# First slab by contraction unit for all four row tiles, from an x laid out turned, behind 36 small matmuls

## The chip, the cores and the metric

One core of a Trainium2 chip runs the whole program. The metric is the device time of one execution in microseconds. TensorE does matmuls, VectorE and ScalarE do the elementwise work, SyncE and ScalarE issue the DMAs.

## The reference

Two transformer blocks run after one another on x (512 tokens x 1024, f32). What matters here is the head of the first block:

```
xn   = rmsnorm(x, attn_norm_g)              # x * rsqrt(mean(x*x)) * g, per token
proj = xn @ w_in                            # 1024 -> 2312 columns
qa, ka, va, qb, kb, vb, f_logit = split(proj, (512, 128, 128, 512, 512, 512, 8))
qa = rmsnorm(qa per head, q_norm_a);  ka = rmsnorm(ka per head, k_norm_a)
out_a = sliding-window attention of qa, ka, va in blocks of 128 queries
...                                         # second attention, out projection, MLP, second block
```

The per-token factor rsqrt(mean(x*x)) commutes with the product by w_in, so it can be applied to x or, later, to rows of proj.

## The kernel before

Every f32 product is done as three passes in fp32r: each operand is split into a high part (ScalarE copies it to fp32r) and the rest (VectorE subtracts), and TensorE adds high x high, high x low and low x high. Weights come in slabs of up to 512 columns, and a slab in four units `q` of two 128-row blocks (`raw[q]`, 512 KB). A unit is loaded by SyncE (`unit`, L465), its high part is made by ScalarE (`high_of`, L611), its low part by VectorE (`low`, L1702), and the latter's end (`unit_split`) also lets SyncE load the next slab's unit into the same buffer. `gemm_done` counts finished product tiles, `gemm_free` tiles whose bank has been read.

**The first stage**, which the change is about, computes eight tiles of proj, in the order of `FIRST` (L50), (slab, row tile). Slab 0 is qa (512 columns), slab 1 is ka, va and the forget logits (264 columns). At the start the gain vector is spread over the partitions by two f32 matmuls of ones (L1148). VectorE multiplies row tile 0 of x by it, TensorE turns the tile by 8 transposes (`turn_half`, L1124), and both splits are made of the turned tile (`xt_high` L630, `xt_low` L1693). Then `first_product` (L1157) multiplies tile 0 unit by unit as slab 0 arrives, and each further row tile is turned in the middle of the product before it (`between`, L1210). Row tile 0 is scaled late, by `root0`, the others by `first_rows` (L1710) before they are turned.

**After each of the eight tiles** come its heads, each engine in a written order. ScalarE squares the tile (`head_squares`, L664), VectorE sums per head (`head_means`, L1731), ScalarE takes a first root (`head_roots`, L676: a logarithm L680 and an exponential L681) and for slab 1 copies v and the logits (L716, L717), VectorE refines the root and scales the rows into `qn` (`head_rows`, L1740, ends with `gemm_free`). TensorE turns `qn` (`turn_heads`, L1196), and ScalarE stores the result with its gain (`head_gain`, L653, ends with `qk_stored`). In ScalarE's loop (L704) `head_gain(g - 3)` stands ahead of `head_squares(g)`. VectorE's last of these, `head_means(7)`, `maxima(0)` and `head_rows(7)`, stand behind its loop (L1929 to L1931).

**The main loop of the first block** has 70 halves in a fixed order on each engine. On TensorE its first instruction is `scores(0)` (L1254), the scores of the first head pair of query block 0, and what it waits for is not touched by the change:

```
if p == 0:
    pe.wait_ge(gemm_free, 6)
    ...
    pe.wait_ge(silu_step, SINK_STEPS)
...
    if h == 0:
        pe.wait_ge(qk_stored, max(FIRST.index((0, n)), FIRST.index((1, n))) + 1)
```

Behind it TensorE has `part_product` (L1229) of slab 2, three of 24 k steps to each half, and the remaining head turns.

## Time and profile before

| | us |
|---|---|
| median of 3 runs | 1192.47 (1192.09 to 1193.83) |
| span of the profiled execution | 1191.0 |
| TensorE busy | 1175.3 |
| VectorE busy | 702.9 |
| ScalarE busy | 485.0 |

The profiled execution's own time beside its span isn't given apart: the span is from the first to the last instruction, and the median of the runs lies 1.5 us above it. The chain of work that ended last is 91% TensorE. Busy time of TensorE is modelled, so the waits and the spacing of matmuls are read, not the busy share.

### The profile page before, as it was taken

How to read it: one execution, taken by the hardware profiler on the slowest of the kernel's cores; microseconds unless marked ns; L12 is line 12 of the kernel's file. 1: busy time of each engine (PE TensorE's matmuls, PEld its weight loads, DVE VectorE, ACT ScalarE, POOL GpSimd, SP SyncE). 2: the span in 40 equal slices, each digit the busy share in tenths (PEclk: the TensorE clock that was granted, in tenths of full speed). 3: DMA queues.
4: the chain of work that ended last, by engine and by line, in shares of the span. 5: the costliest groups of instructions: out<-in, count | busy, mean ns of one | idle time of the engine just before them, and what ended most of it. 6: DMA issues, size and time to landing. Idle time of an engine off the chain costs nothing.

```text
span 1191.0 us, 16691 instructions
## 1 busy us (share of the span) xinstructions
PE 1175.3 (99%) x6182; PEld 950.3 (80%) x6184; DVE 702.9 (59%) x1081; ACT 485.0 (41%) x874; POOL 24.7 (2%) x23
## 2 busy tenths in 40 slices
PE   8999999999999999999999999999999999999997
PEld 5877776688888888888888886578988888888886
DVE  7786567768777776753688235847633333333335
ACT  6655444535334334324541113845541532432431
POOL 0000000000000000000000003400000000000000
PEclk9999999999999999999999999999999999999999
DMA  6322211218667676644325221132333222223301
GB/s 228 124 72 71 72 36 54 72 64 284 223 213 241 207 254 208 213 145 142 123 72 174 85 71 46 54 126 71 108 105 106 98 97 89 106 88 93 119 19 71
DMA packets 76573, 144.27 MB, mean 121 GB/s; under 512 B 7347, under 2 KB 11315, under 8 KB 76500
## 3 DMA queue, kind: packets, MB, share of 16 engines
q1 hardware_dynamic: 54882, 99.12, 25.3%
q10 hardware_dynamic: 21618, 44.18, 11.6%
q8 instruction: 46, 0.75, 0.3%
q14 instruction: 27, 0.22, 0.1%
HBM read 140.36 MB, written 2.13 MB: 120 GB/s over the span
## 4 chain that ended last, share of the span: by engine, by line
PE 91%; DVE 5%; ACT 2%; issue 1%; DMA 0%; DVEq 0%; ACTq 0%
PE gemm L1091 25%; PE gemm L1093 25%; PE gemm L1092 25%; PE aux L1132 1%; PE aux L1338 1%; PE gemm L1378 1%; PE gemm L1379 1%; PE gemm L1380 1%; DVE nmax L2192 1%; PE aux L1091 1%; PE aux L1615 1%; PE gemm L1275 1%; PE aux L1093 1%; PE aux L1092 1%; PE gemm L1288 1%
## 5 line engine op out<-in xcount | busy, mean ns | idle before, releaser
L1091 PE MATMUL gemm<-xt_hi,w_hi 128*128 128x512 f32 (+1 forms) x704 | 254.4, 361 | 0.3 <-DVE xt_lo L1697 0.3
L1093 PE MATMUL gemm<-xt_hi,w_lo 128*128 128x512 f32 (+1 forms) x704 | 253.7, 360 | 0.0
L1092 PE MATMUL gemm<-xt_lo,w_hi 128*128 128x512 f32 (+1 forms) x704 | 253.5, 360 | 0.0
L1707 DVE TENSOR_TENSOR w_lo<-w_raw,w_hi 128x1024 fp32r<-128x1024 f32 (+1 forms) x176 | 208.0, 1210 | 31.0 <-ACT w_hi L840 26.3
L1091 PE MATMUL gemm<-w_hi,ht_hi 128*128 128x512 f32 (+1 forms) x512 | 198.9, 389 | 0.0
L1093 PE MATMUL gemm<-w_hi,ht_lo 128*128 128x512 f32 (+1 forms) x512 | 198.5, 388 | 0.0
L1092 PE MATMUL gemm<-w_lo,ht_hi 128*128 128x512 f32 (+1 forms) x512 | 198.3, 387 | 0.0
L840 ACT ACTIVATE w_hi<-w_raw 128x1024 fp32r<-128x1024 f32 x124 | 124.0, 1049 | 172.5 <-PE gemm L1093 127.9
L1091 PEld LDWEIGHTS gemm<-xt_hi,w_hi 128*128 128x128 f32 x704 | 132.7, 189 | 21.6 <-DVE xt_lo L1697 0.5
L1092 PEld LDWEIGHTS gemm<-xt_lo,w_hi 128*128 128x128 f32 x704 | 132.7, 188 | 20.1
L1093 PEld LDWEIGHTS gemm<-xt_hi,w_lo 128*128 128x128 f32 x704 | 132.7, 189 | 20.1
L2005 DVE TENSOR_TENSOR ht_lo<-hid,ht_hi 128x512 fp32r<-128x512 f32 x64 | 44.3, 692 | 171.0 <-ACT hid L853 171.0
L1091 PEld LDWEIGHTS gemm<-w_hi,ht_hi 128*128 128x128 f32 x512 | 96.2, 188 | 20.4
L1093 PEld LDWEIGHTS gemm<-w_hi,ht_lo 128*128 128x128 f32 x512 | 96.1, 188 | 19.8
L1092 PEld LDWEIGHTS gemm<-w_lo,ht_hi 128*128 128x128 f32 x512 | 96.2, 188 | 19.7
L848 ACT ACTIVATE relu<-gemm 128x512 f32<-128x512 f32 x64 | 38.3, 599 | 166.5 <-PE gemm L1093 166.5
L2062 DVE SCALAR_TENSOR_TENSOR mod_acc<-wm,csil,mod_acc 128x512 f32<-128x512 f32 x112 | 84.0, 750 | 5.3 <-DMA wm<-in_w_mod 1.6
L1091 PE MATMUL gemm<-w_hi,xt_hi 128*128 128x512 f32 (+1 forms) x208 | 80.3, 386 | 0.4 <-DVE xt_lo L1697 0.4
L1093 PE MATMUL gemm<-w_hi,xt_lo 128*128 128x512 f32 (+1 forms) x208 | 77.9, 374 | 0.0
L1092 PE MATMUL gemm<-w_lo,xt_hi 128*128 128x512 f32 (+1 forms) x208 | 77.6, 373 | 0.0
L604 ACT ACTIVATE w_hi<-w_raw 128x1024 fp32r<-128x1024 f32 (+1 forms) x52 | 51.0, 1021 | 61.2 <-PE gemm L1093 60.0
L2019 DVE TENSOR_TENSOR sub<-sub,gemm 128x512 f32<-128x512 f32 (+1 forms) x24 | 16.2, 677 | 60.5 <-PE gemm L1093 60.4
(271 smaller groups left out, 1412.1 us busy)
## 6 DMA issues: line engine op xcount, KB each, us to landing
wm<-in_w_mod ACTq DMA_DIRECT2D x64, 512.0 KB, 4.7
w_raw<-in_w_in SPq DMA_DIRECT2D x32, 512.0 KB, 4.4
w_raw<-in_w_up SPq DMA_DIRECT2D x32, 512.0 KB, 3.8
w_raw<-in_w_down SPq DMA_DIRECT2D x32, 512.0 KB, 5.6
w_raw<-in_w_mlp_in SPq DMA_DIRECT2D x32, 512.0 KB, 3.8
w_raw<-in_w_mlp_out SPq DMA_DIRECT2D x32, 512.0 KB, 4.4
w_raw<-in_w_out SPq DMA_DIRECT2D x16, 512.0 KB, 3.9
x<-in_x SPq DMA_DIRECT2D x4, 512.0 KB, 6.5
```

Of the source, the lines that this page charges most:

```text
L604: act.activation(w_hi[slot(s)][:, UK * q:UK * (q + 1), 0:width], raw[q][:, :, 0:width], ACT.Copy).then_inc(hi_split, 1)
L840: act.activation(w_hi[s % 2][:, UK * q:UK * (q + 1), :], raw[q][:, :, :], ACT.Copy).then_inc(hi_split, 1)
L848: act.activation(relu[c % 2][:], gp[(t0 + c) % 4][:], ACT.Relu).then_inc(relu_done, 1)
L1091: pe.matmul(bank, lh, rh, start=(k == 0), stop=False)
L1092: pe.matmul(bank, lh, rl, start=False, stop=False)
L1093: mm = pe.matmul(bank, ll, rh, start=False, stop=(k == KT - 1))
L1132: mm = pe.transpose(dst, src, ident[:])
L1275: pe.matmul(bank[e][:, lo:256], q_a[rows[e], h // 2, n * P:(n + 1) * P], k_a[rows[e], swap, (n - 1) * P + lo:(n + 1) * P], start=True, sto ...
L1707: dve.tensor_tensor(w_lo[slot(s)][:, ks, 0:width], raw[q][:, :, 0:width], w_hi[slot(s)][:, ks, 0:width].bitcast(F32), ALU.subtract).then_i ...
L2005: dve.tensor_tensor(ht_lo[:, c, :], hid[c % 2][:], ht_hi[:, c, :].bitcast(F32), ALU.subtract).then_inc(hid_lo, 1)
L2019: dve.tensor_tensor(cols, cols, bank[:], ALU.add).then_inc(gemm_free, 1)
L2062: ins = dve.scalar_tensor_tensor(acc, w, c, acc, ALU.mult, ALU.add)
```

## The change

- **x comes a second time, turned.** The host lays out `x_turned` (2 MB, 128 partitions x 8 k blocks x 512 tokens), and ScalarE's queue loads it in five DMAs, the gain (one column per k block) behind the first. SyncE's queue loads slab 0, its first unit in two halves, then the four row tiles of x, needed for the squares and later for the residual, and the identity.
- **The splits of x** are made directly per k block by ScalarE (`x_high`) and VectorE (`x_low`), with the gain as the per-partition scale. The gain matmuls, the 32 transposes of x and the row scaling leave the first stage. All four row tiles are now scaled late, by `root1(m)`.
- **Slab 0 goes unit by unit for all four row tiles**, into four banks, in the order high x high, low x high, high x low. Tiles 0 to 3 end one after another in the last unit. `FIRST` is reordered: the four tiles of slab 0 come first, then the four of slab 1. `slot` and `slab_end` follow.
- **The squares of x** and their roots stand behind the splits of slab 0 on ScalarE, the refinements among the splits of slab 1 on VectorE.
- **Heads:** `head_gain(g - 4)` stands ahead of `head_squares(g)` for g from 4, and `head_gain(4)` behind ScalarE's loop. The splits of slab 2 move to g = 5 and 6 on both engines. `sinks` moves behind g = 4. TensorE turns heads 0, 1, 2, and 3 with 4, in the middle (k = 5) of products 4 to 7.
- **TensorE begins** with 36 bf16 matmuls of ones (128 columns each) into bank `aux[3]`, which nothing reads before it is written again.

The diff, cut to its core ("..." where lines are left out; counts in waits on `xr_ready` and `xr_turned` shift by four tiles):

```diff
 KV_W = 264
-FIRST = ((0, 0), (0, 1), (0, 2), (1, 0), (1, 1), (1, 2), (1, 3), (0, 3))
+FIRST = ((0, 0), (0, 1), (0, 2), (0, 3), (1, 0), (1, 1), (1, 2), (1, 3))
...
-    return 1 - s if s < 2 else s % 2
+    return s % 2
...
+WARM = 36
...
+        x_turned = at("x_turned", [P, KT, S], F32, H)
...
@@ SyncE queue
+            def first_unit():
+
+                c0, width = IN1_COLS[0]
+                for k in range(UK):
+                    sp.dma_start(raw[0][:, k, 0:width], t["w_in"][k * P:(k + 1) * P, c0:c0 + width]
+                                 ).then_inc(first_loaded if k == 0 else raw_loaded[0], 16)
+
+            first_unit()
+            for q in range(1, UQ):
+                unit(q, rows(t["w_in"], 0, q)[:, :, IN1_COLS[0][0]:IN1_COLS[0][0] + IN1_COLS[0][1]], IN1_COLS[0][1], None)
+            for m in range(TT):
+                x_tile(m)
+            small(ident[:], t["c_ident"], ident_loaded)
+
+            for s, (c0, width) in list(enumerate(IN1_COLS))[1:]:
...
@@ ScalarE
-            load(gain_row[:], t["attn_norm_g"].rearrange("(a n) -> a n", a=1), gain1_loaded)
+            for k in range(UK):
+                load(x_turned[:, k, :], t["x_turned"][:, k, :], first_turned if k == 0 else turned_loaded[0])
+                if k == 0:
+                    load(gain1[:], t["attn_norm_g"], gain1_loaded)
+            for q in range(1, UQ):
+                load(x_turned[:, UK * q:UK * (q + 1), :], t["x_turned"][:, UK * q:UK * (q + 1), :], turned_loaded[q])
...
-            first_squares(0)
-            high_of(0, 0)
...
-            high_of(0, 3)
+            def x_high(k):
+
+                act.wait_ge(*x_arrived(k))
+                did(act.activation(xt_hi[:, k, :], x_turned[:, k, :], ACT.Copy, scale=gain1[:, k:k + 1]), xt_hi_done)
+
+            act.wait_ge(gain1_loaded, 16)
+            x_high(0)
+            act.wait_ge(first_loaded, 16)
+            act.activation(w_hi[0][:, 0, :], raw[0][:, 0, :], ACT.Copy).then_inc(first_split, 1)
+            x_high(1)
+            act.wait_ge(raw_loaded[0], 16)
+            act.activation(w_hi[0][:, 1, :], raw[0][:, 1, :], ACT.Copy).then_inc(hi_split, 1)
+            for q in range(1, UQ):
+                x_high(UK * q)
+                x_high(UK * q + 1)
+                high_of(0, q)
+            for m in range(TT):
+                first_squares(m)
+                if m:
+                    first_root(STAT_N1 + m - 1)
+            high_of(1, 0)
+            first_root(STAT_N1 + TT - 1)
+            high_of(1, 1)
...
+                if g < TT:
+                    act.wait_ge(rs_done, 2 * (m + 1))
                 did(act.activation(qsq[:, 0:heads * HD], banks[in_bank(g)][:, 0:heads * HD], ACT.Square,
-                                   **late_root(m)), hsq_done)
+                                   scale=root1(m)), hsq_done)
...
-            first_squares(2)
-            xt_high(NT_1 + 1, 1)
...
-            act.wait_ge(xr_ready, 4)
             load(alibi[:], t["c_alibi"], alibi_loaded)
-
             act.wait_ge(heads_loaded, 16 * 8)

-            for g, (s, m) in list(enumerate(FIRST))[2:]:
-                if g >= 3:
-                    head_gain(g - 3)
-                if g == 7:
-                    high_of(2, 2)
-                    high_of(2, 3)
+            for g, (s, m) in enumerate(FIRST):
+                if g >= 4:
+                    head_gain(g - 4)
+                if g in (5, 6):
+                    high_of(2, 2 * (g - 5))
+                    high_of(2, 2 * (g - 5) + 1)
                 head_squares(g)
-                if g == 6:
-                    high_of(2, 0)
-                    high_of(2, 1)
+                if g == 0:
+                    high_of(1, 2)
+                    high_of(1, 3)
                 head_roots(g)
                 if s == 1:
-                    did(act.activation(v_a[:, m, :], gp[g % 4][:, P:2 * P], ACT.Copy, **late_root(m)), v_copied)
-                    did(act.activation(flog[:, m, :], gp[g % 4][:, 256:KV_W], ACT.Copy, **late_root(m)), v_copied)
+                    did(act.activation(v_a[:, m, :], gp[g % 4][:, P:2 * P], ACT.Copy, scale=root1(m)), v_copied)
+                    did(act.activation(flog[:, m, :], gp[g % 4][:, 256:KV_W], ACT.Copy, scale=root1(m)), v_copied)
+            head_gain(4)
...
@@ TensorE
-            pe.wait_ge(row_ready, 1)
-            pe.wait_ge(gain1_loaded, 16)
...
-            turn_half(NT_1, 1)
...
+            pe.wait_ge(ones_ready, 1)
+            for _ in range(WARM):
+                pe.matmul(aux[3][:, 0:P], ones_full[:], ones_full[:], start=True, stop=True)
+
+            def first_products():
...
+                def step(m, k, lhs, w):
+                    return pe.matmul(gp[m][:], lhs[:, k, m * P:(m + 1) * P], w[0][:, k, :],
+                                     start=(lhs is xt_hi and w is w_hi and k == 0), stop=(w is w_lo and k == KT - 1))

                 pe.wait_ge(xt_hi_done, 1)
+                pe.wait_ge(first_split, 1)
+                for m in range(TT):
+                    step(m, 0, xt_hi, w_hi)
+                pe.wait_ge(xt_lo_done, 1)
+                for m in range(TT):
+                    step(m, 0, xt_lo, w_hi)
+                pe.wait_ge(xt_hi_done, 2)
                 pe.wait_ge(hi_split, 1)
+                for m in range(TT):
+                    step(m, 1, xt_hi, w_hi)
+                pe.wait_ge(first_rest, 1)
+                for m in range(TT):
+                    step(m, 0, xt_hi, w_lo)
+                pe.wait_ge(xt_lo_done, 2)
+                for m in range(TT):
+                    step(m, 1, xt_lo, w_hi)
                 pe.wait_ge(unit_split, 1)
+                for m in range(TT):
+                    step(m, 1, xt_hi, w_lo)
+                for q in range(1, UQ):
+                    ks = (UK * q, UK * q + 1)
+                    pe.wait_ge(xt_hi_done, ks[1] + 1)
+                    pe.wait_ge(hi_split, q + 1)
+                    if q < UQ - 1:
+                        for k in ks:
+                            for m in range(TT):
+                                step(m, k, xt_hi, w_hi)
+                        pe.wait_ge(xt_lo_done, ks[1] + 1)
+                        for k in ks:
+                            for m in range(TT):
+                                step(m, k, xt_lo, w_hi)
+                        pe.wait_ge(unit_split, q + 1)
+                        for k in ks:
+                            for m in range(TT):
+                                step(m, k, xt_hi, w_lo)
+                        continue
+                    pe.wait_ge(xt_lo_done, ks[1] + 1)
+                    pe.wait_ge(unit_split, q + 1)
+                    for m in range(TT):
+                        for k in ks:
+                            step(m, k, xt_hi, w_hi)
+                            step(m, k, xt_lo, w_hi)
+                            mm = step(m, k, xt_hi, w_lo)
+                        mm.then_inc(gemm_done, 1)
...
             def between(g):

-                if g < TT - 1:
-                    turn_rows(NT_1 + g + 1)
...
-                        mid_k=2 if g < TT - 1 else KT // 2)
+                for u in {4: (0,), 5: (1,), 6: (2,), 7: (3, 4)}[g]:
+                    if u == 0:
+                        pe.wait_ge(ident_loaded, 16)
+                    turn_heads(u)
+
+            first_products()
+            split_ready(1)
+            for g, (s, m) in list(enumerate(FIRST))[TT:]:
+                product(g, gp[g % 4], tokens(xt_hi, xt_lo, m), w_cols(s, KV_W), KV_W, mid=lambda: between(g), mid_k=5)
...
@@ VectorE
-            def first_rows(m):
+            def x_low(k):
+
+                dve.wait_ge(*x_arrived(k))
+                dve.wait_ge(xt_hi_done, k + 1)
+                did(dve.scalar_tensor_tensor(xt_lo[:, k, :], x_turned[:, k, :], gain1[:, k:k + 1],
+                                             xt_hi[:, k, :].bitcast(F32), ALU.mult, ALU.subtract), xt_lo_done)
+
+            dve.wait_ge(gain1_loaded, 16)
+            x_low(0)
+            dve.wait_ge(first_split, 1)
+            dve.tensor_tensor(w_lo[0][:, 0, :], raw[0][:, 0, :], w_hi[0][:, 0, :].bitcast(F32),
+                              ALU.subtract).then_inc(first_rest, 1)
+            x_low(1)
+            dve.wait_ge(hi_split, 1)
+            dve.wait_ge(first_rest, 1)
+            dve.tensor_tensor(w_lo[0][:, 1, :], raw[0][:, 1, :], w_hi[0][:, 1, :].bitcast(F32),
+                              ALU.subtract).then_inc(unit_split, 1)
+            for q in range(1, UQ):
+                x_low(UK * q)
+                x_low(UK * q + 1)
+                low(0, q)
+            for m in range(TT):
+                mean_square(STAT_N1 + m, STAT_N1 + m + 1)
+            low(1, 0)
+            for m in range(TT):
                 refine(STAT_N1 + m)
-                scaled(NT_1 + m, STAT_N1 + m, x[:, m, :], gain1[:])
-
...
-            refine(STAT_N1)
+            low(1, 1)
...
+                    return dve.scalar_tensor_tensor(dst, src, root1(m), scale, ALU.mult, ALU.mult)
...
-            mean_square(STAT_N1 + 2, STAT_N1 + 3)
-            xt_low(NT_1 + 1, 1)
...
-            first_rows(3)
             dve.wait_ge(heads_loaded, 16 * 8)
             did(dve.tensor_scalar(gains[:, 0:1], gains[:, 0:1], QSCALE, None, ALU.mult), silu_step)
             did(dve.tensor_scalar(gains[:, 2:3], gains[:, 2:3], QSCALE, None, ALU.mult), silu_step)
-            head_rows(0)
-            low(1, 2)
...
-            for g in range(2, PHASE - 1):
+            for g in range(PHASE - 1):
                 head_means(g)
-                if g == 6:
-                    low(2, 0)
-                    low(2, 1)
+                if g == 0:
+                    low(1, 2)
+                    low(1, 3)
+                if g in (5, 6):
+                    low(2, 2 * (g - 5))
+                    low(2, 2 * (g - 5) + 1)
                 head_rows(g)
+                if g == 4:
+                    sinks()
...
-            low(2, 2)
-            low(2, 3)
             head_means(PHASE - 1)
...
@@ host
+        "x_turned": np.ascontiguousarray(f("x", (S, D)).T.reshape(KT, P, S).transpose(1, 0, 2)), "w_in": f("w_in"), "b_forget": f("b_forget"),
```

## Rows read from the trace of the kernel before

**Rows 1.** The page: the span, and the chain that ended last, by engine.
```profile
span 1191.0 us, 16691 instructions
...
PE 91%; DVE 5%; ACT 2%; issue 1%; DMA 0%; DVEq 0%; ACTq 0%
```

**Rows 2.** TensorE's timeline, 0 to 52 us: start, us, line, out<-in, shape, count, [idle before].
```profile
8.87 2.31 PE L1162 MATMUL gemm<-w_hi,xt_hi 128*128 128x512 f32 x4
...
24.08 0.39 PE L1092 MATMUL gemm<-w_lo,xt_hi 128*128 128x512 f32 x1
...
27.03 0.40 PE L1093 MATMUL gemm<-w_hi,xt_lo 128*128 128x512 f32 x1
...
34.23 0.28 PE L1092 MATMUL gemm<-w_lo,xt_hi 128*128 128x264 f32 x1
...
36.89 0.29 PE L1093 MATMUL gemm<-w_hi,xt_lo 128*128 128x264 f32 x1
...
51.19 0.49 PE L1275 MATMUL gemm<-k_a,q_a 64*128 64x128 f32 x4
```

**Rows 3.** Whole span, what TensorE waited for: us in total, times, longest.
```profile
PE aux L1132 <- DVE xt_lo L1697: 2.0, 1, 2.0
```

**Rows 4.** ScalarE's timeline, the first microseconds.
```profile
4.54 1.06 ACT L618 ACTIVATE junk<-x 128x1024 bf16<-128x1024 f32 x1 [2.50 <-DMA x<-in_x]
...
6.01 1.06 ACT L604 ACTIVATE w_hi<-w_raw 128x1024 fp32r<-128x1024 f32 x1 [0.33 <-DMA w_raw<-in_w_in]
7.15 0.20 ACT L623 ACTIVATE st<-st 128x1 f32<-128x1 f32 x1
...
8.22 0.60 ACT L634 ACTIVATE xt_hi<-aux 128x512 fp32r<-128x512 f32 x1 [0.63 <-PE aux L1132]
...
10.43 1.06 ACT L618 ACTIVATE junk<-x 128x1024 bf16<-128x1024 f32 x1
...
11.61 1.06 ACT L604 ACTIVATE w_hi<-w_raw 128x1024 fp32r<-128x1024 f32 x1
```

**Rows 5.** VectorE's timeline, 20 to 54 us.
```profile
20.83 1.33 DVE L1707 TENSOR_TENSOR w_lo<-w_raw,w_hi 128x528 fp32r<-128x528 f32 x2
...
24.64 0.27 DVE L1674 TENSOR_SCALAR st<-st 128x1 f32<-128x1 f32 x1
...
33.92 0.16 DVE L1776 CAST sink_parts<-sink 1x8 bf16<-1x8 f32 x1
...
35.59 0.69 DVE L1735 TENSOR_REDUCE hst<-qsq 128x8 f32<-128x512 f32 x1
...
38.45 0.29 DVE L1735 TENSOR_REDUCE hst<-qsq 128x2 f32<-128x128 f32 x1
...
41.31 0.29 DVE L1735 TENSOR_REDUCE hst<-qsq 128x2 f32<-128x128 f32 x1 [0.25 <-ACT qsq L673]
...
43.98 0.29 DVE L1735 TENSOR_REDUCE hst<-qsq 128x2 f32<-128x128 f32 x1 [0.34 <-ACT qsq L673]
...
46.44 0.29 DVE L1735 TENSOR_REDUCE hst<-qsq 128x2 f32<-128x128 f32 x1
...
51.04 2.36 DVE L1707 TENSOR_TENSOR w_lo<-w_raw,w_hi 128x1024 fp32r<-128x1024 f32 x2
53.32 0.68 DVE L1735 TENSOR_REDUCE hst<-qsq 128x8 f32<-128x512 f32 x1
54.03 0.17 DVE L1737 TENSOR_SCALAR hst<-hst 128x8 f32<-128x8 f32 x1
```

**Rows 6.** ScalarE's timeline, behind the seventh tile.
```profile
48.28 0.18 ACT L680 ACTIVATE hst<-hst 128x2 f32<-128x2 f32 x1
...
49.25 0.48 ACT L659 ACTIVATE k_a<-aux,gains 128x256 f32<-128x256 f32 x1
```

**Rows 7.** Stretches, at the start and behind the 2 us wait: busy by engine, granted clock, DMA share, GB/s.
```profile
3.00:4.00 1.00, 0.66 (x1) 0.49 (x2) 0.00 (x0) 0.00 (x0) 0.00 (x0) 1.00 1.03 410
247.00:252.00 5.00, 5.00 (x20) 4.07 (x20) 4.12 (x7) 0.60 (x1) 0.00 (x0) 0.66 0.34 105
```

More of the change, by code:

```diff
@@ L329, in build @@
         gains = place("gains", [P, 4], F32)
+        gain1 = place("gain1", [P, KT], F32)
         cvec = place("cvec", [P, 2, KT], F32)
@@ L412, in build, with x_arrived @@
         qn_turned, qk_stored = sem("qn_turned"), sem("qk_stored")
-        row_ready, gain_spread, gain_copied, first_half, gain_copied_act = (sem(n) for n in (
-            "row_ready", "gain_spread", "gain_copied", "first_half", "gain_copied_act"))
+        turned_loaded = [sem(f"turned_loaded{q}") for q in range(UQ)]
+        first_turned, first_loaded = sem("first_turned"), sem("first_loaded")
+        def x_arrived(k):
+            return (first_turned if k == 0 else turned_loaded[k // UK], 16)
         v_copied, k_scaled, f_turned, f_step, f_act = (sem(n) for n in (
@@ L1142, in turn_rows @@
                     turn_half(n, half, permute)
-            pe.wait_ge(row_ready, 1)
-            pe.wait_ge(gain1_loaded, 16)
-            for half in range(2):
-                pe.matmul(gp[2 + half][:], ones_row[:], gain_row[:, half * NC:(half + 1) * NC],
-                          start=True, stop=True).then_inc(gain_spread, 1)
-            pe.wait_ge(ident_loaded, 16)
-            pe.wait_ge(first_half, 1)
-            turn_half(NT_1, 0)
-            pe.wait_ge(xr_ready, NT_1 + 1)
-            turn_half(NT_1, 1)
@@ L1939, in _ @@
                         dve.wait_ge(gemm_done, g + 1)
-                        if g == 16:
-                            did(dve.tensor_scalar(v_b[:, 0, :], banks[in_bank(g)][:], root0, None, ALU.mult), gemm_free)
-                        else:
-                            did(dve.tensor_copy(v_b[:, g % 4, :], banks[in_bank(g)][:]), gemm_free)
+                        did(dve.tensor_scalar(v_b[:, g % 4, :], banks[in_bank(g)][:], root1(g % 4), None, ALU.mult),
+                            gemm_free)
                 if h % 2 == 0:
```

127 lines of the change are left out of this document (11 added, 116 removed).

## The prediction

> **What bounds the kernel now.** I read the page, TensorE's waits, then the timelines of TensorE, ScalarE and VectorE up to the first attention scores. By the page the last-ending chain is 91% TensorE [rows 1]; behind the start TensorE's longest wait in the whole span is 2.0 us [rows 3]. So a shift of the stage before the main loop should reach the end nearly undiminished: weights, heads and splits behind it move along. The place to read is one instruction, the first score matmul (L1275), which starts at 51.19 [rows 2]. Useful products began at 8.87 [rows 2]. Between the two TensorE works almost without a gap, but the other engines don't rest: VectorE ends `head_means` of the eighth tile at 54.20 (54.03 + 0.17) [rows 5], 3 us after the scores have started. The reader should see two clocks in this stage, TensorE's products and the chain of heads on VectorE and ScalarE. Today the scores need only the first, and a part of the second.
>
> **TensorE's side after the change.** Matmuls of 512 columns follow one another in (27.03 - 24.08) / 13 = 0.227 us, those of 264 in (36.89 - 34.23) / 22 = 0.121 [rows 2]. Data: the first 512 KB were in ScalarE's hands at 4.54, the next at 6.01, so 1.47 us for 512 KB [rows 4]. The first pieces of x_turned and of the weights are 256 KB each and land together at about 4.54. `x_high` is an operation of 0.60 [rows 4], half a unit's high part likewise, so the first product starts at 4.54 + 1.2 = 5.8 in place of 8.87. Slab 0 is 96 matmuls, 96 x 0.227 = 21.8 us, to 27.6. A unit of both operands (1 MB) arrives in 2.9 us and is worked on for 5.5, so behind the first no unit is late. The gain matmuls and the transposes of x are gone from here. Slab 1 is 96 x 0.121 = 11.6 plus five head turns. If nothing held it, TensorE would reach the scores near 41.
>
> **The clock at the start.** The first four products took 2.31 us from 8.87 [rows 2], more than twice 4 x 0.227: 512 columns at the 1.2 GHz level, although the column of the granted clock says 1.00 there [rows 7]. The 36 small matmuls run while TensorE would wait for data, so their own time costs nothing. What they may save is at most some 3 us of products at the lower level, what they may fail to save is as much. I count neither, because the last unit's first tile (27.6 - 3 x 1.36 = 23.5) isn't what its heads wait for, as the next part shows; up to 2 or 3 us are hidden there.
>
> **The other side: what the scores now wait for.** `scores(0)` waits for `qk_stored` of the later of (0, 0) and (1, 0) in `FIRST`. That was the fourth tile, it is now the fifth, and `head_gain(4)` is written behind ScalarE's whole loop. Ahead of it on ScalarE stand squares, roots and copies of all eight tiles, and the roots of the eighth wait for `head_means(7)`, VectorE's last. So the scores now wait for all of VectorE's heads. Step by step:
> - The last unit of both operands is the eighth piece of 512 KB: 4.54 + 7 x 1.47 = 14.8. ScalarE makes two `x_high` and a high part, 0.63 x 2 + 1.06: 17.1.
> - Four squares at 11.61 - 10.43 = 1.18 [rows 4], three roots of two operations of 0.20 with their gaps, 0.48: 6.2 us, to 23.3. A high part of slab 1 (264 columns wide), some 0.6: 23.9.
> - VectorE: low part of slab 1, unit 0, half of 1.33 [rows 5]; four refinements, each 0.27 plus a small one, 0.5: 2.0; unit 1, 0.66; two gain columns, 0.4. To 27.6.
> - Heads of the wide tiles: one round took 38.45 - 35.59 = 2.86 [rows 5], of which some 0.65 is the wait for ScalarE's root. Head 0 has two narrow low parts (1.33) in that wait: 3.5. Heads 1 to 3: 8.6. To 39.7.
> - Head 4, narrow, 43.98 - 41.31 = 2.67, then the sinks, 35.59 - 33.92 = 1.67 [rows 5]: 44.0.
> - Heads 5 and 6, each with two low parts of slab 2: the same round took 51.04 - 46.44 = 4.60 [rows 5]. Twice: 53.2. `head_means(7)`, narrow, 0.5: 53.7.
> - ScalarE from its root to the end of a narrow `head_gain`: 49.25 + 0.48 - 48.28 = 1.45 [rows 6], and a hand-over of 0.1 on each side: 55.4.
>
> A check on this sum: before, `head_means(7)` ended at 54.20, here at 53.7. VectorE loses the row scaling and the later splits of x, but starts its heads later, and has seven of them behind it instead of racing beside TensorE. The work is about the same; what is new is that the scores wait for its end. TensorE itself: product 4 waits for `head_rows(0)` (`gemm_free`) until 31.1, four products with turns take 4 x 2.9 + 1.6 = 13.2, so it stands at `scores(0)` from 44.3 to 55.4, 11 us with nothing to do. The scores start 55.4 - 51.19 = 4.2 us later than before.
>
> **The clock behind that wait.** After the 2.0 us wait [rows 3] the granted clock fell: its mean over 247 to 252 is 0.66 [rows 7], so (1 - 0.66) / 0.5 = 0.68 of 5 us, 3.4 us, at the 1.2 GHz level, which loses 1.7 us of work. The wait here is five times longer, and it stands ahead of dense products of slab 2. I take 2.0, with 0 and 4 as ends: 0 if the clock holds, 4 if twice that stretch is slow. The Trainium skill (TensorE: Matmul & The Clock Gate, Part 1: The HAM clock gate) holds half rate to be the default state, released by activity alone. By that rule the first scores start cold at once, and the price can't be 0; by the column at the start alone, which says 1.00 on a TensorE that has done nothing, it would be, and the sum would end 2.0 lower.
>
> **Costed at nothing.** The two more scaled squares and row scalings on the slower form, some hundredths of a us each, are in the rounding. The reloads of slab 2 start when slab 1's low parts are made, near 24 to 29, and are needed from 42. The row tiles of x end with the twelfth piece, 4.54 + 11 x 1.47 = 20.7, for the last square at 21.6: a cover of 0.9 us only, which a rival below takes up. Behind the scores VectorE has less left than before (one narrow `head_rows` instead of two low parts and a wide head), but TensorE did not wait there before, so nothing comes back.
>
> **Sum.** 1191.0 + 4.2 + 2.0 = 1197.2 of span. The median of the runs lies 1.5 above the span: 1198.7.
>
> **Rivals.**
> - **The chain of heads does not decide; TensorE's gain comes through (faster).** The place is `scores(0)`, the condition that ScalarE's `head_gain(4)` is done before TensorE gets there. For it: products start 3 us sooner, gain matmuls and transposes are gone. If only the products counted, scores at 44.3: -6.9 and no cold clock, 1185.6. If `gemm_free` of the sixth tile counted (44.0 + 4.6 = 48.6): -2.6 and part of the clock's price, about 1191. It decides from a chain over 4 us shorter than my sum; but the round times are this trace's own, the same work ended at 54.20 before. 0.08.
> - **Break-even.** The chain comes 3 us shorter and the clock costs 1 or less: within 2 us of before. 0.05.
> - **Data late (slower still).** x_turned, weights and then x share the DMA engines. In 3 to 4 us one queue alone already had them at 1.03 of their time, 410 GB/s [rows 7], so the second queue can't bring more. If the mix runs 10% slower, x ends at 22.3, past its cover of 0.9, and the chain is 0.7 us later; the small loads of the heads, queued behind x, can add a further one, and a first product late by 1 us doesn't matter. With 3 to 4 us of clock price: 1201 to 1203. 0.17.
> - **The small matmuls run, and are unread.** If they did not raise the clock, nothing changes at the scores; that part alone then has no effect. It is inside the forecast.
>
> **Numbers.** Forecast 0.70 (1196 to 1201), late data 0.17, break-even 0.05, faster 0.08. The range leaves out the faster rival and the far tail: 1195 to 1203. A measurement of this kernel tells 0.2% (2.4 us) from no change. Faster 0.08, same 0.06, slower 0.86.
>
> **What would show it.** The first product near 5.8 to 6.5; `gemm_done` of tile 0 near 24 to 25; VectorE's `head_means(7)` near 53.7; one TensorE wait of about 11 us ahead of L1275's scores, put down to ScalarE's store of k_a; the scores at 55 to 56; granted clock at 0.5 for some 3 to 5 us behind. From there the two traces should run in parallel, some 6 us apart. It is wrong if the scores start before 51.2, if TensorE's wait is put down to something else, or if the lag at 200 us differs from that at 62 us.

## The result, and the profile after

The median after is 1201.02 us (1200.80 to 1201.80, 4 runs), before it was 1192.45 on the same chip (1192.09 to 1193.83, 4 runs): ratio 1.0071, 95% interval 1.0058 to 1.0083, so 8.6 us slower. The profiled execution has a span of 1200.0, 9.0 more than before [rows 1].

The page of the kernel after, its first line and the chain that ended last:

```profile
span 1200.0 us, 16693 instructions
...
PE 88%; DVE 5%; ACT 2%; SPq 2%; issue 2%; DMA 0%; ACTq 0%; DVEq 0%
```

Then what TensorE waited for over the whole span (us in total, times, longest):

```profile
PE gemm L1284 <- ACT k_a L683: 11.0, 1, 11.0
PE gemm L1160 <- ACT w_hi L662: 2.0, 1, 2.0
PE gemm L1098 <- DVE qn L1764: 2.0, 1, 2.0
PE aux L1139 <- DVE xt_lo L1705: 2.0, 1, 2.0
```

One new wait stands out, 11.0 us ahead of the first scores, put down to ScalarE's store of k_a. The fourth line is the 2.0 us wait of before [rows 3], unchanged. TensorE's timeline (start, us, line, tiles, count, [idle before]) shows both ends of the stage:

```profile
1.10 4.02 PE L1154 MATMUL aux<-ones_full 128*128 128x128 bf16 x36 [1.10 <-DVE ones_full L1662]
7.17 1.17 PE L1160 MATMUL gemm<-w_hi,xt_hi 128*128 128x512 f32 x4 [2.04 <-ACT w_hi L662]
8.17 1.53 PE L1160 MATMUL gemm<-w_hi,xt_lo 128*128 128x512 f32 x4
9.50 1.91 PE L1160 MATMUL gemm<-w_hi,xt_hi 128*128 128x512 f32 x4
...
57.72 0.80 PE L1284 MATMUL gemm<-k_a,q_a 64*128 64x128 f32 x4 [11.04 <-ACT k_a L683]
65.58 0.49 PE L1284 MATMUL gemm<-k_a,q_a 64*128 64x128 f32 x4
...
89.32 0.70 PE L1284 MATMUL gemm<-k_a,q_a 64*128 64x256 f32 x4
```

Products begin 1.7 us sooner than before (7.17 against 8.87 [rows 2]), and the scores 6.5 us later (57.72 against 51.19 [rows 2]). For the second and the sixth scores, the kernel before has

```profile
56.54 0.49 PE L1275 MATMUL gemm<-k_a,q_a 64*128 64x128 f32 x4
...
80.51 0.70 PE L1275 MATMUL gemm<-k_a,q_a 64*128 64x256 f32 x4
```

so the lag is 65.58 - 56.54 = 9.0 at the second scores, 89.32 - 80.51 = 8.8 at the sixth, and near 220 us still 8.7. Everything is lost before 66 us. The chain that the scores waited for, on VectorE:

```profile
27.65 0.69 DVE L1750 TENSOR_REDUCE hst<-qsq 128x8 f32<-128x512 f32 x1
...
30.73 0.71 DVE L1715 TENSOR_TENSOR w_lo<-w_raw,w_hi 128x528 fp32r<-128x528 f32 x1 [1.45 <-ACT w_hi L617]
...
32.74 0.69 DVE L1750 TENSOR_REDUCE hst<-qsq 128x8 f32<-128x512 f32 x1
...
34.27 0.17 DVE L1668 TENSOR_TENSOR hst<-hst 128x8 f32<-128x8 f32 x1 [0.64 <-ACT hst L705]
...
41.53 0.29 DVE L1750 TENSOR_REDUCE hst<-qsq 128x2 f32<-128x128 f32 x1
...
46.36 0.29 DVE L1750 TENSOR_REDUCE hst<-qsq 128x2 f32<-128x128 f32 x1 [0.57 <-ACT qsq L697]
...
51.20 0.29 DVE L1750 TENSOR_REDUCE hst<-qsq 128x2 f32<-128x128 f32 x1 [0.71 <-ACT qsq L697]
...
55.67 0.17 DVE L1752 TENSOR_SCALAR hst<-hst 128x2 f32<-128x2 f32 x1
```

and on ScalarE, at its start and at its end:

```profile
5.64 0.72 ACT L657 ACTIVATE xt_hi<-x_turned,gain 128x512 fp32r<-128x512 f32 x1 [3.61 <-DMA gain<-in_attn_norm_g]
...
16.18 1.06 ACT L617 ACTIVATE w_hi<-w_raw 128x1024 fp32r<-128x1024 f32 x1
...
30.05 0.65 ACT L617 ACTIVATE w_hi<-w_raw 128x528 fp32r<-128x528 f32 x1 [1.85 <-DMA w_raw<-in_w_in]
...
57.10 0.47 ACT L683 ACTIVATE k_a<-aux,gains 128x256 f32<-128x256 f32 x1
```

Each head starts when the one before it ends, so the chain goes at VectorE's pace. VectorE idles in it for a late weight unit (1.45 us, at 30.73), for ScalarE's late squares (0.57 and 0.71, at 46 and 51), and in each of rounds 1 to 4 some 0.64 us for ScalarE's root, as at 34.27; in rounds 5 and 6 the low parts of slab 2 fill that last wait. The windows behind the wait (busy of PE, PEld, DVE, ACT, POOL, then granted clock, DMA share, GB/s):

```profile
57.00:59.00 2.00, 1.28 (x9) 1.08 (x10) 0.14 (x1) 0.55 (x2) 0.00 (x0) 0.50 0.25 93
...
61.00:63.00 2.00, 2.00 (x7) 1.48 (x6) 0.00 (x0) 0.00 (x0) 0.00 (x0) 0.50 0.00 0
63.00:66.00 3.00, 3.00 (x17) 2.27 (x16) 1.59 (x3) 1.85 (x3) 0.00 (x0) 0.97 0.00 0
```

TensorE ran at the 1.2 GHz level for some 5.3 us behind the scores' start, to about 63.0.

### The profile page after: what moved, and what is told of

Same layout as the page of the kernel before. It is cut to its first block, busy times and chain, and to the rows that moved or that the text cites. A ratio compares the mean times of both kernels' runs of the same rounds, so it can differ in the third digit from the quotient of the medians.

```text
span 1200.0 us, 16693 instructions
## 1 busy us (share of the span) xinstructions
PE 1170.9 (98%) x6182; PEld 950.3 (79%) x6184; DVE 698.8 (58%) x1075; ACT 487.3 (41%) x874; POOL 24.7 (2%) x23
## 4 chain that ended last, share of the span: by engine, by line
PE 88%; DVE 5%; ACT 2%; SPq 2%; issue 2%; DMA 0%; ACTq 0%; DVEq 0%
PE gemm L1098 24%; PE gemm L1099 24%; PE gemm L1100 24%; PE aux L1347 1%; SPq L458 1%; PE aux L1139 1%; PE gemm L1387 1%; PE gemm L1389 1%; PE gemm L1388 1%; PE aux L1592 1%; PE aux L1098 1%; PE gemm L1284 1%; PE aux L1624 1%; PE aux L1100 1%; PE aux L1099 1%
## 5 line engine op out<-in xcount | busy, mean ns | idle before, releaser
L2002 DVE TENSOR_TENSOR ht_lo<-hid,ht_hi 128x512 fp32r<-128x512 f32 x64 | 44.3, 692 | 171.0 <-ACT hid L860 171.0
L1098 PE MATMUL gemm<-w_hi,xt_hi 128*128 128x512 f32 (+1 forms) x184 | 71.5, 388 | 2.0 <-DVE qn L1764 2.0
L1100 PE MATMUL gemm<-w_hi,xt_lo 128*128 128x512 f32 (+1 forms) x184 | 69.1, 376 | 0.0
L1099 PE MATMUL gemm<-w_lo,xt_hi 128*128 128x512 f32 (+1 forms) x184 | 68.9, 375 | 0.0
```

The source lines that it names most:

```text
L1098: pe.matmul(bank, lh, rh, start=(k == 0), stop=False)
L1099: pe.matmul(bank, lh, rl, start=False, stop=False)
L1100: mm = pe.matmul(bank, ll, rh, start=False, stop=(k == KT - 1))
L2002: dve.tensor_tensor(ht_lo[:, c, :], hid[c % 2][:], ht_hi[:, c, :].bitcast(F32), ALU.subtract).then_inc(hid_lo, 1)
```

## The experiments

The theory was that of the prediction: the scores now wait for the whole chain of heads, and the clock falls behind that wait. Open were the size of each, whether the small matmuls and the late loads count, and whether the new order can be had without the wait. All medians stand against runs of the kernel before on the same chip. The chips differ between some of the experiments, and the 95% intervals of the ratios are 1 to 2 us wide to either side. So a difference of 2 us or less between two edited kernels isn't clear of noise by the medians alone, and is read together with the traces.

**1. The stores that the scores wait for, earlier.**

```diff
-                if g >= 4:
-                    head_gain(g - 4)
+                for u in {4: (0,), 5: (1, 2), 6: (3, 4)}.get(g, ()):
+                    head_gain(u)
...
-            head_gain(4)
```

> The changed kernel (1201.0 us), with ScalarE's head_gain(4) moved out from behind its loop: gains 1 and 2 stand ahead of the squares of tile 5, gains 3 and 4 ahead of those of tile 6. Nothing else moves. Theory A (the scores wait for the store of k_a, which is written behind all heads): the scores then wait only for gemm_free of the sixth tile, which the changed kernel had at 50.5 us, so they start near 50.6 in place of 57.7, TensorE's wait shrinks from 11.0 to some 4 to 5 us, the clock still falls, and the time is 7 us shorter, about 1194. Rival B (VectorE's whole chain of heads is the limit, whatever the scores wait for): TensorE stops again a few us later, at the products of slab 2 or the head turns, for gemm_free of tiles 7 and 8 (55.3 and later), and the gain is 2 to 3 us, about 1198. Rival C (the lost time is in the start, in late data and the slow clock of the first products): no change.

Measured: 1199.03 (1198.11 to 1199.25), ratio 1.0051 (1.0034 to 1.0068). TensorE's waits, 0 to 80 us:

```profile
PE gemm L1097 <- DVE qn L1763: 6.1, 2, 4.6
PE gemm L1283 <- DVE qn L1763: 4.6, 1, 4.6
```

and its timeline there:

```profile
50.70 0.49 PE L1283 MATMUL gemm<-k_a,q_a 64*128 64x128 f32 x4 [4.56 <-DVE qn L1763]
...
56.04 0.79 PE L1097 MATMUL gemm<-w_hi,xt_hi 128*128 128x512 f32 x1 [4.60 <-DVE qn L1763]
```

The wait for k_a is gone, and 2.0 us were won, no more: rival B's result, where theory A asked for 7. The scores waited for `gemm_free` of the sixth tile, and the first product of slab 2 behind them for that of the seventh, both at the end of `head_rows` on VectorE. So `head_gain(4)` is only the last of three waits on one chain. The scores even started 0.5 us sooner than in the kernel before (50.70 against 51.19), and the kernel was still 6.3 us slower: the start of the scores alone doesn't tell the time.

**2. Only the wait, put into the kernel before.**

```diff
-                if g >= 3:
+                if 3 <= g < 7:
                     head_gain(g - 3)
...
+            head_gain(4)
...
-                        pe.wait_ge(qk_stored, max(FIRST.index((0, n)), FIRST.index((1, n))) + 1)
+                        pe.wait_ge(qk_stored, 5 if n == 0 else max(FIRST.index((0, n)), FIRST.index((1, n))) + 1)
```

> The kernel before (1192.5 us) with this part of the change alone: head_gain(4) stands behind ScalarE's loop of heads and scores(0) waits for it. x, loads, order of tiles and products stay as they were. Theory A: VectorE ends head_means of the eighth tile near 54.2 as before, ScalarE needs 1.5 to 1.9 us from there, so the scores start near 56 in place of 51.2, 4.9 us later, behind a wait of some 5 us, and the clock falls behind it, 1.7 to 2.5 us more: about 1199. Rival C (the loss of the change lies in its start): within 1 us of before, since ScalarE has slack.

Measured: 1199.14 (1198.27 to 1199.33), ratio 1.0055 (1.0038 to 1.0071). The wait, the second scores, and a window behind the wait:

```profile
PE gemm L1276 <- ACT k_a L659: 4.1, 1, 4.1
```

```profile
62.36 0.49 PE L1276 MATMUL gemm<-k_a,q_a 64*128 64x128 f32 x4
```

```profile
57.00:60.00 3.00, 3.00 (x10) 2.32 (x9) 0.35 (x3) 0.51 (x3) 0.00 (x0) 0.50 0.11 43
```

With nothing else of the change in the kernel, the store behind the loop costs 6.4 us by the medians, where the whole change costs 8.6. In the trace the scores start at 55.43, 4.2 us later than before, and the second ones 5.8 us later, so the clock adds 1.6. In the changed kernel the scores start 2.3 us later than here: VectorE's chain ends at 55.84 in place of 54.23, and ScalarE copies v and the logits of the last tile, now one of slab 1, between its root and the store (0.37 and 0.27 us).

**3. Without the small matmuls.**

```diff
-WARM = 36
+WARM = 0
```

> The changed kernel without the 36 small matmuls. If they raise the clock earlier: the first products run longer at 1.2 GHz, tile 0 ends up to 2 us later than 26.7. Theory A says the chain of heads then starts later by what exceeds VectorE's own readiness (it took up the first tile at 27.65, tile 0 ended at 26.8, so 0.2 us of room behind ScalarE's squares): up to 2 us slower, 1201 to 1203. If they do nothing for the clock: 1201.0, no change. It is faster only if the small matmuls themselves delayed the first product, which the wait of 2.0 us behind them speaks against.

Measured: 1200.64 (1199.88 to 1200.79), ratio 1.0067 (1.0050 to 1.0084): as with them. The start did change:

```profile
7.26 2.05 PE L1160 MATMUL gemm<-w_hi,xt_hi 128*128 128x512 f32 x4 [7.26 <-ACT w_hi L662]
9.10 1.91 PE L1160 MATMUL gemm<-w_hi,xt_lo 128*128 128x512 f32 x4
```

Against 1.17 and 1.53 with them. The first tile's last unit begins 1.2 us later (26.40 against 25.22), and so do its heads on VectorE, but not those of the second:

```profile
28.81 0.69 DVE L1750 TENSOR_REDUCE hst<-qsq 128x8 f32<-128x512 f32 x1 [1.20 <-ACT qsq L697]
...
32.36 0.69 DVE L1750 TENSOR_REDUCE hst<-qsq 128x8 f32<-128x512 f32 x1
```

In the changed kernel these stand at 27.65 and 32.74. Head 0 there waits 1.45 us for slab 1's last unit, and here for nothing but its tile: the later start fits into the room that the late unit leaves. (The unit is also issued 1.5 us sooner in this trace, at 23.39 in place of 24.86, so the two traces don't differ in the block alone.) Where the unit isn't late, as in run 7, VectorE waits 1.39 us for tile 0, and the start isn't free.

What the block does for the clock also differs from trace to trace. TensorE's code up to the first products is the same in the changed kernel and in runs 1 and 4 to 8, and its pause behind the block is 1.9 to 2.5 us in all seven. Yet the first four products took 1.17, 2.05, 1.17, 1.34, 1.85, 2.04 and 1.16 us; in runs 4 and 8 the later ones ran at full speed too, in the changed kernel and in run 5 they slowed down. One trace with the block and one without don't show what it is worth.

**4. The clock price alone.** 190 more small matmuls into a free bank fill the wait before the scores.

```diff
+            pe.wait_ge(qk_stored, 2)
+            for _ in range(190):
+                pe.matmul(aux[1][:, 0:P], ones_full[:], ones_full[:], start=True, stop=True)
```

> The changed kernel with 190 more matmuls of ones (128 columns, bf16) into bank aux[1] ahead of scores(0), behind a wait for head_gain(1), which frees the bank: TensorE is busy through its 11 us wait. If the price of the wait is its length plus a clock that has fallen (theory A: 6.5 us plus 2.5 us), the scores still start near 57.7, the products behind them run at full clock, and the time is 2.5 us shorter, 1198.5. If the 2.5 us have another cause (other waits behind the scores), no change; if the small matmuls run beyond the wait, slower by the excess, at most 1 us at full clock.

Measured: 1198.99 (1197.84 to 1199.76), ratio 1.0052 (1.0035 to 1.0069). The granted clock stayed at 1.00, and the timeline reads

```profile
57.92 0.49 PE L1284 MATMUL gemm<-k_a,q_a 64*128 64x128 f32 x4
...
63.28 0.49 PE L1284 MATMUL gemm<-k_a,q_a 64*128 64x128 f32 x4
```

ScalarE's store of k_a, in the same trace:

```profile
56.26 0.47 ACT L683 ACTIVATE k_a<-aux,gains 128x256 f32<-128x256 f32 x1
```

From the scores to the second scores it is 63.28 - 57.92 = 5.36 us, as in the kernel before (56.54 - 51.19 = 5.35), against 65.58 - 57.72 = 7.86 in the changed kernel: the price of the clock is 2.5 us. The medians give 2.0. The scores start no sooner, but not because k_a is late: its store ends at 56.73, and the small matmuls run some 1 us beyond it.

**5. The late unit.** Of the seventeen small loads that stand ahead of and between slab 1's units on SyncE's queue, the eight head gains go ahead of all units and the nine others behind them.

```diff
+                    for args in small_loads[:8]:
+                        small(*args)
                     for q in range(UQ):
                         src = rows(t["w_in"], 0, q)
-                        for args in small_loads[5 * q:5 * (q + 1)]:
-                            small(*args)
...
+                    for args in small_loads[8:]:
+                        small(*args)
```

> The changed kernel (1201.0 us) with SyncE's small loads moved: the eight of the head gains stay ahead of slab 1, the nine others go behind its last unit. In the changed kernel the last unit of slab 1 was not there when ScalarE came to it (1.85 us of waiting, VectorE 1.45 us ahead of head 0's second low part). Theory A (all of VectorE's heads stand ahead of the scores, each wait among them counts in full): the scores start 1.4 to 1.5 us sooner, near 56.2, and the time is 1199.5. Rival: the wait was hidden by the wait for tile 0's product or is replaced by another late load: no change, 1201.

Measured: 1199.87 (1199.46 to 1200.23), ratio 1.0061 (1.0045 to 1.0076); the scores stood at 56.28. In the trace the 1.45 us in which VectorE waited at 30.73 are gone and the scores stand 1.44 us sooner. By the medians it is 1.15 us, and the two intervals of the ratio overlap, so how much of it reaches the end is not shown.

**6. Slab 2's low parts on GpSimd**, its high parts one per round (on top of 1).

```diff
+            for q in range(UQ):
+                pool.wait_ge(raw_loaded[q], 16 * 4)
+                pool.wait_ge(hi_split, 8 + q + 1)
+                ks = slice(UK * q, UK * (q + 1))
+                pool.tensor_tensor(w_lo[0][:, ks, :], raw[q][:], w_hi[0][:, ks, :].bitcast(F32),
+                                   ALU.subtract).then_inc(unit_split, 1)
```

> e1 (1199.0 us) with slab 2's splits out of VectorE's rounds: ScalarE makes one high part in each of the rounds 3 to 6, GpSimd the four low parts (2.36 us each by its rows further on in this kernel). Theory B (behind the store of k_a, VectorE's chain of heads is the limit: gemm_free of tiles 6 and 7): rounds 5 and 6 take 2.65 in place of 4.8 us, gemm_free of the seventh tile comes 4.3 to 4.6 us sooner, and the time is 1194.5. If something else sets the start of slab 2's products (the splits themselves, or the clock), the gain is under 2 us: over 1197.

Measured: 1202.02 (1201.36 to 1202.26), ratio 1.0078 (1.0062 to 1.0093), the slowest of all. A miss (1194.5 was expected), explained by two timelines of the same time, GpSimd's and VectorE's:

```profile
43.92 2.37 POOL L572 TENSOR_TENSOR w_lo<-w_raw,w_hi 128x1024 fp32r<-128x1024 f32 x1 [2.86 <-ACT w_hi L623]
47.88 2.37 POOL L572 TENSOR_TENSOR w_lo<-w_raw,w_hi 128x1024 fp32r<-128x1024 f32 x1 [1.58 <-ACT w_hi L623]
```

```profile
44.21 2.10 DVE L1672 TENSOR_TENSOR hst<-hst 128x2 f32<-128x2 f32 x1 [0.66 <-ACT hst L711]
46.34 0.16 DVE L1673 TENSOR_TENSOR hst<-hst 128x2 f32<-128x2 f32 x1
...
47.89 2.38 DVE L1793 CAST sink_parts<-sink_rest 1x8 bf16<-1x8 f32 x1
```

In these rows a VectorE operation that takes 0.16 us elsewhere lasts until GpSimd's ends. Four such meetings cost 2.16 + 2.10 + 2.38 + 2.07, less 0.66 for the four alone: 8.0 us on the chain, to save four low parts of 1.2. The Trainium skill (SBUF — State Buffer, Who interferes with whom) says that a VectorE instruction with two SBUF inputs contends with a GpSimd instruction that reads SBUF, and that the one that issues later blocks fully. VectorE's row at 44.21 agrees, 2.10 us, for a tensor_tensor with two inputs; the cast at 47.89 has one, which that section lets contend only in a 2-port mode, and the trace doesn't show the mode.

**7. All of it on VectorE, spread.** 1 and 5 together, slab 2's splits one per round in rounds 3 to 6, the sinks in thirds, in VectorE's waits for ScalarE's roots.

```diff
-                if g in (5, 6):
-                    low(2, 2 * (g - 5))
-                    low(2, 2 * (g - 5) + 1)
+                if 3 <= g < 7:
+                    low(2, g - 3)
+                if 2 <= g < 5:
+                    sinks(g - 2)
                 head_rows(g)
-                if g == 4:
-                    sinks()
```

> e1 with three edits, GpSimd left out: loads as in e5 (-1.45 us on VectorE's chain), slab 2's splits one per round in rounds 3 to 6, where each fills the 0.65 us wait for ScalarE's root (-2.4 us), the sinks in thirds into the root waits of rounds 2 to 4 (-1.7 us). gemm_free of the seventh tile then comes at 49.8 in place of 55.3, 2 us sooner than slab 2's products began before (51.8). TensorE still waits some 5 us in all, so 0 to 1.7 us for the clock: 1190.5 to 1192.5, about the kernel before. If VectorE's chain isn't the limit, it stays over 1195.

Measured: 1194.90 (1193.12 to 1195.09, 11 runs), ratio 1.0013 (1.0004 to 1.0022). That is above the 1190.5 to 1192.5 that were expected, and 4.1 us below run 1, the loads' part of it included (1.2 by run 5). The scores started at 49.31, 1.9 us sooner than in the kernel before, but the first product of slab 2 at 53.05 in place of 51.78, behind a wait of 3.0 us and at the 1.2 GHz level. VectorE's 1.39 us of waiting for tile 0 stand on the chain ahead of it.

**8. As 7, with the low parts on GpSimd** (the edit of 6).

> e7 with slab 2's low parts on GpSimd: gemm_free of the seventh tile near 47.5, 4.3 us sooner than slab 2's products began before, TensorE's waits 2 to 4 us in all. 1188.5 if the clock holds, 1190 if it falls: faster than the kernel before (1192.5). If GpSimd's work slows VectorE's, or its low parts (2.36 us each) come too late for slab 2, 1191 or more.

Measured: 1199.30 (1198.02 to 1199.53), ratio 1.0055 (1.0042 to 1.0069): 4.4 us worse than 7, where 1188.5 to 1190 were hoped for and the rival said 1191 or more. Again a VectorE operation lasts as long as a GpSimd low part beside it, four times (2.18, 2.24 and 2.07 us, and three copies that take 2.73 in place of 0.54).

**9. A leaner chain.** As 7, the four refinements of x's roots in three operations over four columns, slab 2's high parts behind the roots of rounds 2 to 5, its last low part behind head 6, and 60 small matmuls at the start.

```diff
-            for m in range(TT):
-                refine(STAT_N1 + m)
+            dve.wait_ge(rs0_done, TT)
+            us, tmps, mss = (st[:, i, STAT_N1:STAT_N1 + TT] for i in (3, 2, 1))
+            did(dve.tensor_tensor(tmps, mss, us, ALU.mult), rs_done)
+            did(dve.tensor_tensor(tmps, tmps, us, ALU.mult), rs_done)
+            did(dve.scalar_tensor_tensor(us, tmps, 3 / LN_SCALE, us, ALU.add, ALU.mult), rs_done)
...
                 head_roots(g)
+                if 2 <= g < 6:
+                    high_of(2, g - 2)
```

> e7 (1194.9 us) with four edits, each meant to shorten the chain of heads: the four refinements of x's roots as three operations on four columns (0.6 in place of 2.0 us), slab 2's high parts behind the roots of rounds 2 to 5, so that VectorE doesn't wait for them (0.6 us twice), its last low part behind head 6 (1.1 us), and 60 small matmuls at the start in place of 36, so that the first products don't start cold (tile 0 ended at 27.9 in e7, 26.3 at best). Theory B: gemm_free of the seventh tile at 49 in place of 53.0, 2.8 us sooner than slab 2's products began in the kernel before; 1190 if the clock holds, 1191.5 if it falls behind TensorE's remaining waits (some 2 and 1 us): at or below the kernel before (1192.7). If the heads aren't the limit: over 1194.

Measured: 1193.82 (1193.05 to 1194.84, 11 runs), ratio 1.0010 (1.0001 to 1.0019), where 1190 to 1191.5 was expected, and no clear gain over 7. The first products ran at full speed throughout, and head 0 began at 26.14. VectorE now waits for ScalarE, whose high parts and stores stand ahead of the squares:

```profile
44.64 0.29 DVE L1753 TENSOR_REDUCE hst<-qsq 128x2 f32<-128x128 f32 x1 [1.05 <-ACT qsq L699]
...
49.03 0.28 DVE L1753 TENSOR_REDUCE hst<-qsq 128x2 f32<-128x128 f32 x1 [0.86 <-ACT qsq L699]
```

**10. As 9, with 24 and 16 small matmuls** in TensorE's two waits, before and behind `scores(0)`.

> e9 with 24 small matmuls ahead of scores(0) and 16 behind it, in TensorE's waits. If the clock falls in e9: 1 to 2 us faster than e9, near 1190. If it holds in e9: the same as e9, or up to 0.5 us slower where the fill runs past the wait.

Measured: 1193.84 (1192.80 to 1195.01, 11 runs), ratio 1.0012 (1.0002 to 1.0021): no change against 9. 2.15 and 1.35 us of idle were left, and the granted clock was 0.65 from 51 to 53 us and 0.50 from 53 to 55.

**11. ScalarE's round turned about.** As 9.

```diff
+            head_squares(0)
+            high_of(1, 2)
+            high_of(1, 3)
             for g, (s, m) in enumerate(FIRST):
...
                 head_roots(g)
...
+                if g < PHASE - 1:
+                    head_squares(g + 1)
+                if 1 <= g < 5:
+                    high_of(2, g - 1)
+                for u in {3: (0,), 4: (1,), 5: (2, 3, 4)}.get(g, ()):
+                    head_gain(u)
```

> As e9_lean (1193.8 us, span 1192.0), with ScalarE's order of a round turned: the roots of tile g, its copies of v and the logits, the squares of tile g + 1, a high part of slab 2 (now in rounds 1 to 4), and only then the head_gain of turned heads (0 in round 3, 1 in round 4, 2 to 4 in round 5). In e9 VectorE waited 1.05, 0.86 and 0.63 us for ScalarE's squares and roots in rounds 5 and 6, and TensorE 3.5 us for the store of k_a and 2.3 for qn. Theory (the round trip between VectorE and ScalarE sets the scores and the first product of slab 2, and its order on ScalarE can be bettered): VectorE's three waits shrink to 0.3 or less each, head_rows(6) ends near 49.7 in place of 51.6, the scores start near 47.5 in place of 48.67, the first product of slab 2 near 49.8 in place of 51.67; behind that the lag falls by 1.5 to 2: 1191.9 us, span 1190.2, ratio to the kernel before 0.9995, so a tie with it. Rival A (the loop behind is then held by something else, the last low part, maxima(0) or head_rows(7) on VectorE, or the slow clock of the first products): 1193.5 to 1194, no change against e9. Rival B (the stores of head_gain, now all in round 5, delay the roots of round 6 and the turns): 1194.5 or more.

Measured: 1191.62 (1190.91 to 1192.65, 11 runs), ratio 0.9993 (0.9984 to 1.0002). On VectorE the same two operations:

```profile
43.20 0.29 DVE L1754 TENSOR_REDUCE hst<-qsq 128x2 f32<-128x128 f32 x1
...
46.22 0.29 DVE L1754 TENSOR_REDUCE hst<-qsq 128x2 f32<-128x128 f32 x1
...
47.85 0.16 DVE L1669 TENSOR_TENSOR hst<-hst 128x2 f32<-128x2 f32 x1 [1.14 <-ACT hst L707]
```

The waits for the squares are gone; that for round 6's root grew from 0.63 to 1.14, where rival B pointed, since three stores now stand ahead of it. The scores started at 47.42 and the first product of slab 2 at 49.37, 3.8 and 2.4 us sooner than in the kernel before, and the result is a tie with it: the granted clock was 0.50 from 46 to 52 us.

**12. As 11, with 40 and 12 small matmuls** in the two waits that are left.

```diff
+            pe.wait_ge(qk_stored, 2)
+            fill(40)
...
                         scores(p)
+                    if p == 0:
+                        fill(12)
```

> As e11_lean_order (1191.6 us, span 1189.3; one wait of 2.67 us before the scores, one of 0.79 before the first product of slab 2, the clock at the 1.2 GHz level from 46 to about 53), with small bf16 matmuls of ones into an unread bank in those two waits: 40 before scores(0), of 0.06 us each, 2.4 us, and 12 behind it, 0.7 us. Theory (the clock behind the waits is the last cost that is left: some 6 us at half speed with about 1 us of idle in them, 2 to 2.5 us of work lost): the granted clock stays at 1.00 or falls for under 2 us, scores and first product start where they did (47.4, 49.4), the second pair's scores near 53.5 in place of 55.7; 1189.7 us, ratio to the kernel before 0.9975. Rival (as in e10, where 24 and 16 such matmuls left 2.15 and 1.35 us of idle and the median did not move: the clock falls anyway, or what it saves is waited for on VectorE's chain behind it): 1191.3 to 1191.9.

Measured: 1189.67 (1189.35 to 1190.86, 11 runs), ratio 0.9978 (0.9969 to 0.9987): 2.8 us (0.22%) faster than the kernel before, clear of noise, and 11 faster than the change as it stood. TensorE's timeline, then a window:

```profile
44.57 2.40 PE L1395 MATMUL aux<-ones_full 128*128 128x128 bf16 x40
47.38 0.49 PE L1285 MATMUL gemm<-k_a,q_a 64*128 64x128 f32 x4 [0.40 <-ACT k_a L685]
...
54.12 0.49 PE L1285 MATMUL gemm<-k_a,q_a 64*128 64x128 f32 x4
```

```profile
48.00:50.00 2.00, 1.48 (x19) 1.22 (x16) 1.72 (x5) 0.74 (x3) 0.00 (x0) 1.00 0.00 1
```

The scores start as in 11, the second ones at 54.12 in place of 55.72, and the clock holds. With 0.40 and 0.52 us of idle left in the two waits the fill works; in 10, with 2.15 and 1.35, it didn't. The order on ScalarE differs between the two as well, so the length of the idle time wasn't varied alone. Whether the edits of 7, 9, 11 and 12 would also speed up the kernel before, in its own order, wasn't tried.

## Why the prediction was right

Forecast 1198.7 in 1195 to 1203, measured 1201.0. Direction, place and mechanism held; the size fell short by 2.3 us. That puts the result at the upper edge of the forecast's own stretch (1196 to 1201), where the rival of late data begins (1201 to 1203), and a part of that rival did happen.

- **The place.** Held. One wait, put down to the store of k_a, 11.0 us as predicted. That the length fits so well is partly luck: it was predicted from 44.3 to 55.4 and came from 46.7 to 57.7, both ends 2.3 to 2.4 us late, since the late head 0 delays product 4 (32.85 in place of 31.1) as well as the scores. Run 2 shows that a wait at this place, put alone into the kernel before, costs 6.4 us; there it is 4.1 us long.
- **The first product** came at 7.17, not 5.8. The gain of x, not the data, was last, at 5.64, and `x_high` took 0.72, not 0.60. The prediction counted on 512 KB per 1.47 us and on no small load. Slab 0's last high part still ended at 17.2 (17.1 predicted), and the first head began at 27.65 (27.6).
- **The start, counted at nothing.** Right, but not for the reason given. The prediction had tile 0 done at 23.5 and up to 2 or 3 us of room ahead of its heads. It was done at 26.7, ScalarE stood 1.9 us waiting for it, and VectorE took up the squares 0.1 us after they were ready, so that room was used up. What hid a still later start in run 3 was the late weight unit behind it.
- **The chain of heads** ended at 55.84, predicted 53.7. This is the term that was mis-sized. Head 0 took 5.09 in place of 3.5, because slab 1's last unit was late; heads 1 to 3 took 8.79 (8.6); head 4 and the sinks 4.83 (4.34, with 0.57 of waiting for ScalarE's squares); rounds 5 and 6 8.99 (9.2). The prediction priced late data at 0.7 to 1.7 in a rival and named the small loads there, for a different unit: x past its cover of 0.9 us, which wasn't late. The loads on SyncE's queue made slab 1's last unit late instead, and in run 5's trace moving them takes 1.44 us off the chain. The last step was 0.2 short too: from `head_means(7)` to the scores 1.88 us in place of 1.7.
- **The clock.** Predicted 2.0, measured 2.5 (lag 9.0 less 6.5); run 4's trace gives 2.5 as well, and its median 2.0.
- **The rule on the clock** (the Trainium skill, TensorE: Matmul & The Clock Gate, Part 1) that the half rate is the default: the trace agrees. The first scores behind the wait took 0.80 us at a granted clock of 0.50, and 0.49 at 1.00 in run 4, where TensorE had been busy up to them; so the prediction's other reading, by which the price would be 0, was wrong. The column misleads at the start: in run 3 it says 1.00 from 7 to 13 us, while four products of 512 columns took 2.05 us.
- **No recovery.** The lag is 8.8 at the sixth scores and 8.7 near 220 us. That the two traces run in parallel was predicted; the distance was to be some 6 us.
- **The faster rival** priced the change by the start of the scores: 1185.6 with scores at 44.3, about 1191 at 48.6. The runs don't bear that out. Scores at 50.70 came with 1199.0 (run 1), at 48.67 with 1193.8 (run 9) and at 47.42 with 1191.6 (run 11), since the first product of slab 2 waits for one tile more and the clock falls. Only with the clock kept up (run 12) was the kernel 0.22% faster.
- **What the prediction didn't say** is that behind the wait for k_a stood two others, `gemm_free` of the sixth and of the seventh tile. Its "-2.6" for the sixth was worked out, but not that the seventh holds slab 2's first product. So undoing the store's place alone seemed worth 7 us (run 1's theory A), and gave 2.

## What to carry to other kernels

Starting an engine's work earlier is worth only what the chain beside it can follow: ask which engine's last operation the next stage waits for, and list all waits on that chain, since removing the one that the profile names shows the next. Where the chain bounces between two engines, put into each round trip the work that fits its wait, and order each engine so that what the other needs next comes first. From run 1 to run 11 that was worth 7.4 us, with no work removed but a few small operations; moved loads and more small matmuls at the start are in that sum. A wait ahead of dense matmuls costs more than its length (here 1.6 us more behind 4.1 us, 2.5 more behind 11.0), and in these runs a filler paid only where it left almost no idle time. And a cost that is hidden behind another one comes back when that one is removed: the start was free until the late unit was gone.

## What was not expected of the hardware

- A GpSimd tensor_tensor of 2.4 us held up VectorE operations of 0.16 us until its own end (2.07 to 2.38 us, in run 6 beside each of its four low parts).
- The same block of 36 small matmuls with a pause of 1.9 to 2.5 us behind it left the first four products at full speed in three of seven traces (1.16 to 1.17 us) and slower in four (1.34 to 2.05). With 60 of them and a pause of 0.7 to 1.2 us (runs 9 to 12) the first products ran at full speed in all four.
- Nine loads of at most 256 KB, between slab 1's units, took SyncE's queue 0.24 to 1.47 us each to issue, 4.9 us in all. Behind the units (run 5) slab 1's last unit was issued at 19.44 in place of 24.86, and the scores stood 1.4 us sooner.
